# Mixing weights and the second layer's norm column, turned in 32x32 blocks on VectorE instead of on TensorE

## The reference, cut to what matters

```python
h = rmsnorm(x, g_mix[l])
proj = h @ w_in[l]
u_a, v_a, q, k, v_b, g_a, g_b = jnp.split(proj, SPLITS, axis=-1)
y_a = spatial_gating(u_a, v_a, sgu_g[l], sgu_w[l], sgu_b[l])
y_b = diff_attention(q, k, v_b, lam, lam_init, rel_bias, sub_g[l])

def spatial_gating(u, v, g_norm, w_s, b_s):
    v = rmsnorm(v, g_norm)
    vc = v.reshape(bsz, s // CHUNK, CHUNK, A_GROUPS, A_GROUP_DIM)
    mixed = jnp.einsum('gts,bnsgc->bntgc', w_s, vc) + b_s.T[None, None, :, :, None]
    return u * mixed.reshape(bsz, s, A_WIDTH)
```

## Time and profile before

| | us |
|---|---|
| median of 3 runs | 1705.21 |
| lowest, highest | 1704.89, 1705.42 |
| the profiled execution | 1704.73 |
| its span, first to last instruction | 1702.9 |
| TensorE busy | 1694.6 (100%) |
| VectorE busy | 967.0 (57%) |
| ScalarE busy | 744.0 (44%) |
| GpSimd busy | 663.7 (39%) |

### The profile page before, as it was taken

The page is one execution under the profiler, slowest core; times in us unless marked ns, Lnnn a source line. Parts: engine busy times, 40 slices in busy tenths (PEclk is TensorE's granted clock), DMA queues, the critical chain, the costliest instruction groups (busy, mean ns, idle before and its releaser), DMA issues.

```text
span 1702.9 us, 22218 instructions
## 1 busy us (share of the span) xinstructions
PE 1694.6 (100%) x7865; PEld 1413.8 (83%) x7865; DVE 967.0 (57%) x1561; ACT 744.0 (44%) x1344; POOL 663.7 (39%) x806
## 2 busy tenths in 40 slices
PE   9999999999999999999999999999999999999998
PEld 7888888888888888888888888888888888888886
DVE  5778866433337766731136788755433476677612
ACT  5666653222345444432256667432223444444222
POOL 3444333333344444434344334324333544444232
PEclk9999999999999999999999999999999999999999
DMA  7322222223232222232352222322242232222322
GB/s 259 125 75 77 93 80 98 99 84 141 96 99 99 99 99 93 91 100 93 100 190 91 83 75 75 119 80 88 85 148 99 76 122 99 94 92 87 110 93 81
DMA packets 146710, 173.93 MB, mean 102 GB/s; under 512 B 2976, under 2 KB 130642, under 8 KB 146130
## 3 DMA queue, kind: packets, MB, share of 16 engines
q1 hardware_dynamic: 146514, 172.96, 30.3%
q10 hardware_dynamic: 128, 0.09, 0.0%
HBM read 166.73 MB, written 6.31 MB: 102 GB/s over the span
## 4 chain that ended last, share of the span: by engine, by line
PE 99%; DVE 0%; ACT 0%; issue 0%; POOL 0%; POOLq 0%; ACTq 0%
PE bank L1475 25%; PE bank L1476 25%; PE bank L1477 25%; PE bank L1510 3%; PE bank L1511 3%; PE bank L1512 3%; PE bank L1737 2%; PE bank L1735 2%; PE bank L1736 2%; PE bank L1533 2%; PE bank L1560 2%; PE bank L1635 1%; PE bank L1544 1%; PE bank L1406 1%; PE bank L1456 1%; PE bank L1665 0%
## 5 line engine op out<-in xcount | busy, mean ns | idle before, releaser
L501 POOL TENSOR_TENSOR w_lo<-raw,w_hi 128x256 fp32r<-128x256 f32 x776 | 628.4, 843 | 1004.0 <-ACT w_hi L563 1004.0
L1475 PE MATMUL bank<-xg_hi,w_hi 128*128 128x512 f32 x1344 | 525.9, 391 | 0.0
L1476 PE MATMUL bank<-xg_lo,w_hi 128*128 128x512 f32 x1344 | 523.3, 389 | 0.0
L1477 PE MATMUL bank<-xg_hi,w_lo 128*128 128x512 f32 x1344 | 523.1, 389 | 0.0
L1477 PEld LDWEIGHTS bank<-xg_hi,w_lo 128*128 128x128 f32 x1344 | 252.3, 188 | 53.1
L1475 PEld LDWEIGHTS bank<-xg_hi,w_hi 128*128 128x128 f32 x1344 | 252.4, 188 | 52.3 <-issue 1.0
L1476 PEld LDWEIGHTS bank<-xg_lo,w_hi 128*128 128x128 f32 x1344 | 252.5, 188 | 51.6 <-issue 1.0
L992 DVE TENSOR_TENSOR w_lo<-raw,w_hi 128x768 fp32r<-128x768 f32 (+2 forms) x146 | 125.0, 856 | 188.7 <-ACT w_hi L562 188.5
L563 ACT ACTIVATE w_hi<-raw 128x1280 fp32r<-128x1280 f32 (+2 forms) x147 | 194.0, 1320 | 0.0
L562 ACT ACTIVATE w_hi<-raw 128x768 fp32r<-128x768 f32 (+2 forms) x147 | 110.4, 751 | 179.9 <-PE bank L1477 90.4
L823 ACT ACTIVATE conv<-up,conv_par 128x512 f32<-128x512 f32 x88 | 71.8, 816 | 129.2 <-DVE up L1254 129.1
(11 more groups left out here) (185 smaller groups left out, 2586.3 us busy)
## 6 DMA issues: line engine op xcount, KB each, us to landing
raw<-in_w_in SPq DMA_DIRECT2D x55, 1024.0 KB, 5.0
raw<-in_w_up SPq DMA_DIRECT2D x44, 1024.0 KB, 5.0
raw<-in_w_br SPq DMA_DIRECT2D x16, 1024.0 KB, 4.8
raw<-in_w_down SPq DMA_DIRECT2D x12, 1024.0 KB, 4.9
raw<-in_w_out SPq DMA_DIRECT2D x8, 1024.0 KB, 4.8
raw<-in_w_down SPq DMA_DIRECT2D x8, 896.0 KB, 4.5
x_spill<-x_res SPq DMA_DIRECT2D x2, 2048.0 KB, 7.6
x_res<-x_spill SPq DMA_DIRECT2D x2, 2048.0 KB, 9.3
```

The costliest lines, as they stand in the source:

```text
L501: last = nc.gpsimd.tensor_tensor(w_lo[p_][:, k, :], raw[p_][:, k, :], f32(w_hi[p_][:, k, :]), ALU.subtract)
L1475: nc.tensor.matmul(out, w_hi[w][:, k, cols], x_hi[:, a, :], start=first and k == 0, stop=False)
L1476: nc.tensor.matmul(out, w_hi[w][:, k, cols], x_lo[:, a, :], start=False, stop=False)
L1477: mm = nc.tensor.matmul(out, w_lo[w][:, k, cols], x_hi[:, a, :], start=False, stop=last and k == kt - 1)
```

## The change

Both turns leave TensorE and become block transposes on VectorE. Sixteen instructions turn a layer's mixing weights: for each block of 32 rows `a` and each block of 32 columns `c`, one instruction turns the block of all eight matrices, from `sgu_raw` straight to `sgu_t`. In layer one, three of the four `a` come at VectorE's step 4 and the last at step 6, behind the evacuation of the first half of the queries; in layer two all four come at step 4. ScalarE's copies go, and the first logits and SyncE now wait for the fourth `a`. In layer two, four block transposes turn the norm row at step 2 into a new buffer `rms_turn`, and the column is read from there.

```diff
@@ sync
                     if (p, n) == (1, 0):
-                        sp.wait_ge(sguw_t, l * 2 + 2)
+                        sp.wait_ge(sguw_t, l * 4 + 4)
                         sp.wait_ge(bias_out, 16)
@@ scalar
-                if i == 5:
-                    for b in range(2):
-                        sc.wait_ge(sguw_t, l * 2 + b + 1)
-                        nc.scalar.activation(sgu_t[:, 4 * b:4 * b + 4, :],
-                                             bank[LOGIT + b][:, :].rearrange("p (g t) -> p g t", g=4), ACT.Copy)\
-                          .then_inc(sguw_ok, 1)
@@ vector
+            def turn_mixing_weights(a):
+
+                if a == 0:
+                    ve.wait_ge(sguw_in, l * 16 + 16)
+                    ve.wait_ge(rms_ok, 2 * l + 1)
+                for c in range(4):
+                    last = nc.vector.transpose(sgu_t[32 * c:32 * c + 32, :, 32 * a:32 * a + 32],
+                                               sgu_raw[32 * a:32 * a + 32, :, 32 * c:32 * c + 32])
+                last.then_inc(sguw_t, 1)
+
@@ vector, the loop over i
                 evac_round(0, i // 2, i % 2)
+                if i == 4:
+                    for a in range(3 + l):
+                        turn_mixing_weights(a)
+                if l == 0 and i == 6:
+                    turn_mixing_weights(3)
                 if l and i == 2:
+                    for c in range(4):
+                        rows = slice(32 * c, 32 * c + 32)
+                        last = nc.vector.transpose(rms_turn[rows, :, :],
+                                                   rms[rows, :].rearrange("p (t c q) -> p t c q", t=TOK, c=4)[:, :, c, :])
+                    last.then_inc(rms_t, 1)
                     ve.wait_ge(rms_t, l)
-                    nc.vector.tensor_copy(rms_col[:, :], bank[HEAD][:, :].rearrange("p (t q) -> p t q", t=TOK)[:, :, 0])\
-                      .then_inc(rms_col_ok, 1)
+                    nc.vector.tensor_copy(rms_col[:, :], rms_turn[:, :, 0]).then_inc(rms_col_ok, 1)
@@ tensor
                     if a % UNITS == 0:
-                        pe.wait_ge(sguw_ok, l * 2 + 2)
+                        pe.wait_ge(sguw_t, l * 4 + 4)
-                    if l and (n, half) == (1, 0):
-                        pe.wait_ge(rms_ok, 2 * l + 1)
-                        for t in range(TOK):
-                            mm = nc.tensor.transpose(bank[HEAD][:, t * P:(t + 1) * P], rms[:, t * P:(t + 1) * P], ident[:, :])
-                        mm.then_inc(rms_t, 1)
-                    if n == 2 and half == 0:
-                        pe.wait_ge(sguw_in, l * 16 + 16)
-                        for g in range(GROUPS):
-                            mm = nc.tensor.transpose(bank[LOGIT + g // 4][:, (g % 4) * P:(g % 4 + 1) * P], sgu_raw[:, g, :],
-                                                     ident[:, :])
-                            if g % 4 == 3:
-                                mm.then_inc(sguw_t, 1)
```

More of the change, by code:

```diff
@@ L179, in encoder_kernel @@
     head_rms = sb("head_rms", 194, [P, 4])
+    rms_turn = sb("rms_turn", 194.25, [P, TOK, 32])
     sgu_raw = sb("sgu_raw", 167, [P, GROUPS, P])
@@ L249, in encoder_kernel @@
     bias_in, sguw_in, sgu_in = sem("bias_in"), sem("sguw_in"), sem("sgu_in")
-    sguw_t, sguw_ok = sem("sguw_t"), sem("sguw_ok")
+    sguw_t = sem("sguw_t")
     qk_done, biased, max_ok, exp_ok = sem("qk_done"), sem("biased"), sem("max_ok"), sem("exp_ok")
```

## The result

The kernel after takes 1707.51 us (median of 15 runs, 1705.96 to 1711.71), the kernel before 1705.21 (15 runs): ratio 1.0015, 95% interval 1.0008 to 1.0022, so 1.4 to 3.8 us more. The profiled execution of after took 1706.63 (span 1704.8), 1.90 more than that of before; 1706.6 was forecast for it.

The account below looks back on a forecast made before the run. TensorE was taken to bound the kernel, with 99% of the chain. Layer one's 3.17 less layer two's 1.31 gave +1.86 us on the profiled 1704.73, so 1706.6; the median, 0.48 above that execution, 1707.1; range 1703.0 to 1709.9.

Parts of the forecast that it names:

- A block transpose, 0.444 us: VectorE: each 32x256 transpose takes 0.444 us, by the line through the 32x128 and 32x1024 rows; bounds 0.31 and 0.62.
- the rival of dearer transposes: Each 0.1 us more per transpose delays SyncE's wait 1.6 us; at 0.62 the time is 1709.9; chance 0.14.
- Keys and queries: Layer one, VectorE: twelve transposes move the keys' second evacuation and the steps after it by 1.66 us.
- first pause: Layer one: TensorE waits about 1.8 us ahead of the first logits, for the first queries' low parts ending at 56.87.
- second pause: Layer one: TensorE idle some 2 us ahead of the first product with the values, released by ScalarE's turned block.
- SyncE's queue: Layer one: wait for the last transposes delays bias table (out 53.63) and slot 5 (54.29); slot 5's split 3.7 us late.
- Layer one, +3.17: TensorE 3.17 us later at the first product with the values, its saved 0.87 and the first pause included.
- The term for the restart: Layer one: about 0.1 us (0.11 in the sum) lost in the products behind TensorE's wait at the values.
- Layer two, -1.31: Layer two gives 0.44 + 0.87 = 1.31 us clean, with 2.4 us of room left for slot 5.
- The norm column's cover: Layer two: four transposes, 1.24 us, fit VectorE's 1.27 gap before 876.20; without that cover, up to 1.24 lost.
- The covered wait: Rival: slot 5 there by 59.9, TensorE never waits at 74.65, full 2.18 us stand: 1703.0; chance 0.14.
- The rival of a slower clock behind a pause: TensorE at half pace after the second pause adds 1.6 us: 1708.7; chance 0.06.

Follow-up runs that it names:

- second experiment: Kernel after with the raw mixing weights on other bytes, so SyncE need not wait for the transposes: 1704.70 us, ratio 0.9997.
- third experiment: Kernel after with slot 5's load issued ahead of SyncE's wait, the bias table still behind it: 1706.38 us, ratio 1.0006.

## Why the prediction was right

- **A block transpose, 0.444 us.** 5.40 for twelve and 7.23 for sixteen are 0.45 each. The line through the two shapes of before held, and the rival of dearer transposes fell. The Trainium skill (VectorE: DVE Perf Modes, The DRAIN you can't avoid) would have given 0.61 by the estimate of the prediction. Twelve instructions, the last of which alone takes 0.42 to 0.44, fit into 5.40 us only if one starts every 0.45, so no such gap shows here. The 311 ns that the prediction takes from the Trainium skill (VectorE: DVE Perf Modes, The three transpose paths) stand there for a 128x128 tile in bf16; no run here tests that figure.
- **Keys and queries.** Evacuation at 46.74 (46.93 said), low parts of the queries ending at 56.68 (56.87). The first pause is 1.46 us where 1.8 was said. Its size does not count: the chain of after doesn't contain it, since the second pause sets the end by a time of its own. The second experiment, where only the first pause is left, shows what it costs by itself.
- **SyncE's queue.** Issues at 53.39 and 53.85 (53.63 and 54.29 said), first softmax step 59.94 (59.8), split of slot 5 62.88 (62.9), turned block ending at 77.67 (77.67), product with the values 77.73 (77.71). Three small misses cancel here: slot 3's split, on which all that follows hangs, began at 37.05 instead of 37.29 and so brought the table's issue 0.24 earlier; the two issues are 0.46 apart, not 0.66; and slot 5 landed 9.00 after its issue, not 8.6. Not in the prediction: the wait of 0.24 for GpSimd at 70.85, which the second pause swallows too, and that the table alone holds ScalarE and VectorE for most of the delay (third experiment).
- **Layer one, +3.17.** Measured 3.04: 1.46 + 0.24 + 1.94 of pauses, some 0.3 in slower first matmuls behind them (0.34 instead of 0.23 to the next one at 70.85), less 0.87. The term for the restart was too small: 3.08 us by the span's clock at the product with the values, less the 0.29 by which the opening was late, leave 2.79 of the 3.04, so the restart lost some 0.25, not 0.11. That the sum of both layers still came out within 0.1 us of the profiled execution is luck in part.
- **Layer two, -1.31.** Measured -1.4 in after and -1.42 alone. The norm column's cover was exactly used up, with no time lost. Slot 5 went out at 893.88 and the two loads from there landed 8.1 to 9.1 us after issue, by 903.0 at the latest; it was wanted at 904.90, so 1.9 us or more were left (2.4 said).
- **The covered wait.** This rival was priced too low, at 1703.0: it left out the first pause, which stays when the second one is gone. The second experiment is that case and took 1704.70.
- **The clock.** The rival of a slower clock behind a pause fell: the windows of after (core's us; busy time and count of TensorE, its weight loads, VectorE, ScalarE, GpSimd; granted clock; DMA share; GB/s) show 1.00, 2.4 GHz, around both pauses.

```profile
56.00:58.00 2.00, 1.22 (x9) 1.25 (x10) 1.37 (x2) 0.00 (x0) 1.97 (x3) 1.00 1.05 372
...
76.00:78.00 2.00, 0.27 (x2) 0.27 (x3) 1.93 (x4) 1.87 (x5) 1.81 (x3) 1.00 0.00 0
78.00:80.00 2.00, 2.00 (x15) 1.83 (x15) 1.99 (x2) 1.21 (x6) 2.00 (x3) 1.00 0.03 8
```

The median came out 0.4 above the forecast while the profiled execution met it. The runs of after spread over 5.75 us, and what spreads them was not settled.

## What to carry to other kernels

When a step moves to a later place or another engine, look first for who waits for it to free a buffer: here a wait in the DMA queue, moved by 13.6 us, cost more than the 16 instructions that caused it cost by themselves, and the load behind it came 11.5 us late. Work that leaves the bounding engine is free only in the idle stretches of the engine that takes it, and these have to be read one by one from its timeline: the same sixteen transposes cost 3.04 us in layer one or gained 0.97, by their places, the bytes of one buffer and the place of one wait. A pause that ends at a time set elsewhere swallows the pauses before it: the 24.3 us from the table's issue to the product with the values are the same whatever the first pause was. So taking away the first of two pauses should show nothing until the later one is gone; that was not tried by itself.

## What the runs showed of the hardware

TensorE's clock can change behind a pause. In the run with doubled transposes it waited 5.05 us for the first queries; its windows (columns as above) show the grant fall to 0.50, 1.2 GHz, and come back between 68 and 70, and its timeline shows matmuls of 512 columns 0.43 us apart where 0.23 is usual:

```profile
60.00:62.00 2.00, 0.00 (x0) 0.00 (x0) 1.97 (x6) 1.95 (x4) 2.00 (x4) 1.00 0.00 0
62.00:64.00 2.00, 0.00 (x0) 0.00 (x0) 1.95 (x3) 1.30 (x3) 2.00 (x3) 0.50 0.39 99
...
66.00:68.00 2.00, 2.00 (x6) 1.59 (x6) 0.00 (x0) 0.00 (x0) 0.00 (x0) 0.50 1.05 339
68.00:70.00 2.00, 2.00 (x8) 1.59 (x7) 1.38 (x2) 0.06 (x1) 0.00 (x0) 0.79 1.07 376
```

```profile
64.09 0.55 PE L1551 MATMUL bank<-k_hi,q_st 128*128 128x256 f32 x1 [5.05 <-DVE q_st L998]
...
66.37 0.63 PE L1494 MATMUL bank<-xg_lo,w_hi 128*128 128x512 f32 x1
66.79 0.63 PE L1495 MATMUL bank<-xg_hi,w_lo 128*128 128x512 f32 x1
```

It cost nothing there, as TensorE waited once more at 84.69, 1.44 us by 86.36.

Block transposes follow one another every 0.45 us in after, where each writes other partitions than the one before it, and each lasts 0.42 to 0.44. In the run with doubled transposes they follow one another every 0.39: the second of a pair, which reads the same block and writes the same partitions of the other buffer, starts 0.36 after the first, before its 0.42 are over (43.37 and 43.73), and the next pair, on other partitions, starts when the second is over (43.73 + 0.39, 44.13). That the partitions make the difference was not tried.

And the opening isn't the same in every execution: in that run eight matmuls of the high parts took 3.78 us (from 8.60) where after took 2.27 (from 7.51), and slot 2 began 3.57 us later, with a granted clock of 1.00 in the windows of both. Seven of the 50 runs of before beside the experiments lie at 1708.5 to 1708.7, the others at 1704.2 to 1705.4; a late opening would be that size, but none of the seven was profiled.
